# A branch hint at the top of every loop of a fused encoder layer

## The reference

```
mod = silu(c) @ w_mod + b_mod;  sh1, sc1, g1, sh2, sc2, g2 = split(mod, 6)
h = modulate(rms_norm(x), sh1, sc1)
u, q, k, v, f_logit = split(h @ w_in)
q, k = rms_norm(q) * q_gain, rms_norm(k) * k_gain
logf = log_sigmoid(f_logit + b_f)
pool_y = pool_mixer(u, ...)                       # trailing means, windows 2/4/8/16
s = q @ k.T / 8 + F[t] - F[s], masked             # F = cumsum(logf)
att = softmax(s) @ v
x = x + g1 * (concat(pool_y, att) @ w_out)
h2 = modulate(rms_norm(x), sh2, sc2)
y = x + g2 * (square(relu(h2 @ w_up)) @ w_down)
```

## Time and profile before

| | |
|---|---|
| median of 3 runs | 3430.89 us (3429.97 to 3432.27) |
| profiled execution | 3426.77 us, its span 3425.3 us |
| busy | PE 3118.1 us (91%), DVE 2067.2 (60%), ACT 1523.1 (44%), POOL 259.6 (8%) |
| mean granted TensorE clock | 0.953 of 2.4 GHz |

### The profile page before, as it was taken

How to read it: one execution, slowest core, us unless ns; L and a number is a source line. 1 busy time by engine, 2 the same in 40 slices (tenths; PEclk the granted TensorE clock), 3 DMA queues, 4 the chain that set the end, 5 groups by cost and what they waited for, 6 DMA issues and landing times. The chain is left out here.

```text
span 3425.3 us, 51085 instructions
## 1 busy us (share of the span) xinstructions
PE 3118.1 (91%) x17260; PEld 2675.8 (78%) x17260; DVE 2067.2 (60%) x3437; ACT 1523.1 (44%) x2561; POOL 259.6 (8%) x263
## 2 busy tenths in 40 slices
PE   4999998568599999999698899999999999999997
PEld 2999998145478787888486799899899888888886
DVE  3656764533288888889465455655655655565554
ACT  2344443023288888888222344344333333333331
POOL 0000000111111111112000000100100100020001
PEclk7999999689699999999899899999999999999999
DMA  5567565899543434330676643534543632243331
GB/s 193 192 221 247 194 230 179 266 298 320 164 119 84 120 85 106 96 96 12 190 222 196 202 131 127 195 124 129 190 133 124 210 103 92 93 177 117 98 98 50
DMA packets 373365, 532.73 MB, mean 156 GB/s; under 512 B 25488, under 2 KB 305560, under 8 KB 366553
## 3 DMA queue, kind: packets, MB, share of 16 engines
q1 hardware_dynamic: 361421, 487.37, 45.4%
q0 software_dynamic: 11808, 43.79, 3.5%
HBM read 410.69 MB, written 107.95 MB: 151 GB/s over the span
## 5 line engine op out<-in xcount | busy, mean ns | idle before, releaser
L2284 PE MATMUL c_psu<-c_hT,c_up_hi 128*128 128x384 f32 (+1 forms) x2560 | 711.1, 359 | 26.7 <-DVE c_up_lo L2207 19.0
L2284 PEld LDWEIGHTS c_psu<-c_hT,c_up_hi 128*128 128x128 f32 x2560 | 474.2, 189 | 72.9 <-issue 20.3
L2228 DVE TENSOR_TENSOR c_ff<-c_ff,c_psd 128x512 f32<-128x512 f32 x544 | 370.1, 686 | 246.9 <-PE c_psd L2297 244.4
L2284 PE MATMUL c_psu<-c_hT,c_up_lo 128*128 128x384 f32 (+1 forms) x1280 | 458.7, 358 | 0.0
L2168 ACT ACTIVATE c_relu<-c_psu 128x384 f32<-128x384 f32 (+1 forms) x160 | 85.3, 533 | 800.9 <-PE c_psu L2284 800.9
L2297 PE MATMUL c_psd<-c_dn_hi,c_a_hi 128*128 128x512 f32 x1088 | 424.5, 390 | 5.6 <-DVE c_ff L2228 5.6
L2297 PE MATMUL c_psd<-c_dn_hi,c_a_lo 128*128 128x512 f32 x1088 | 425.5, 391 | 0.0
L2297 PE MATMUL c_psd<-c_dn_lo,c_a_hi 128*128 128x512 f32 x1088 | 425.5, 391 | 0.0
L632 PE MATMUL p_psm<-p_whi,p_hT_hi 128*128 128x384 f32 (+1 forms) x952 | 321.8, 338 | 16.8 <-DVE p_wlo L525 10.2
L632 PE MATMUL p_psm<-p_whi,p_hT_lo 128*128 128x384 f32 (+1 forms) x952 | 316.2, 332 | 0.0
L632 PE MATMUL p_psm<-p_wlo,p_hT_hi 128*128 128x384 f32 (+1 forms) x952 | 311.9, 328 | 0.0
(11 more groups left out here) (229 smaller groups left out, 5340.9 us busy)
## 6 DMA issues: line engine op xcount, KB each, us to landing
c_up_raw<-in_w_up_dram SPq DMA_DIRECT2D x80, 1024.0 KB, 5.5
c_dn_raw<-in_w_down_dram SPq DMA_DIRECT2D x80, 1024.0 KB, 4.9
p_raw<-in_w_in_dram SPq DMA_DIRECT2D x24, 1536.0 KB, 7.4
s_krows<-in_cache_k_dram SPq DMA_DIRECT2D x16, 1536.0 KB, 7.0
s_vrows<-in_cache_v_dram POOLq DMA_DIRECT2D x16, 1536.0 KB, 7.7
o_wm<-in_w_mod_dram SPq DMA_DIRECT2D x16, 1024.0 KB, 7.3
q_split<-p_split SPq DMA_DIRECT2D x34, 384.0 KB, 2.3
k_split<-p_split SPq DMA_DIRECT2D x34, 384.0 KB, 2.4
```

What stands on the lines that cost most here:

```text
L2228: dve.tensor_tensor(out, out, ps_d[bank_of(u, p, wide)][:], ALU.add).then_inc(dn_free, 1)
L2284: done = pe.matmul(ps_u[g][:, 0:rows], w[p][:, k, f], x[:, k, 0:rows], start=begin, stop=end)
```

## The change

```diff
+def loop(eng, start, end):
+
+    return eng.bass.Fori(start, end, engines=bass.OrderedEngineSet([eng.engine]), hint_back_edge=True)
...
 def blocks(eng, body):
 
     body(0, 1)
-    with eng.Fori(1, BLOCKS - 1) as b:
+    with loop(eng, 1, BLOCKS - 1) as b:
...
     n = HEADS // 2
     body(0, False)
-    with eng.Fori(1, n - 1) as j:
+    with loop(eng, 1, n - 1) as j:
         body(j, False)
     body(n - 1, True)
...
         def over_steps(eng, b, unit):
 
-            with eng.Fori(0, STEPS // 2 - 1) as i:
+            with loop(eng, 0, STEPS // 2 - 1) as i:
...
```

More of the change, by code:

```diff
@@ L1468, in groups @@
             body(1)
-            with eng.Fori(2, STREAMS) as b:
+            with loop(eng, 2, STREAMS) as b:
                 body(b)
@@ L1786, in over_tiles @@
                 step(0, k)
-            with eng.Fori(1, N // 2 - 2) as i:
+            with loop(eng, 1, N // 2 - 2) as i:
                 for k in range(2):
@@ L2050, in over_blocks @@
         def over_blocks(eng, body):
-            with eng.Fori(0, SMALL) as b:
+            with loop(eng, 0, SMALL) as b:
                 body(b, False, False)
@@ L2099, in body @@
             def body(b, next_wide, last):
-                with sp.Fori(0, STEPS // 2 - 1) as i:
+                with loop(sp, 0, STEPS // 2 - 1) as i:
                     for p in range(2):
@@ L2113, in body @@
                     load_down(first, 0)
-            with sp.Fori(0, SMALL - 1) as b:
+            with loop(sp, 0, SMALL - 1) as b:
                 body(b, False, False)
@@ L2144, in body @@
                     load_x2(b + 1, next_wide)
-            with pool.Fori(0, SMALL - 1) as b:
+            with loop(pool, 0, SMALL - 1) as b:
                 body(b, False, False, False)
```

## The result

The changed kernel is slower: ratio 1.0044 of the kernel before, 95% interval 1.0028 to 1.0060, 15 us; medians of eight runs are 3443.76 us (3436.69 to 3451.45) and 3429.53 us (3420.01 to 3433.95). Its profiled span is 18.1 us longer.

The account below looks back on a forecast made before the run. TensorE carries the time; ScalarE's and VectorE's code stalls at the pair loop's jumps cap the gain at 16.55 us. Terms -8.7 + 0.6 = -8.1 us took the 3430.9 us median to 3423 us, range 3415 to 3442.

Parts of the forecast that it names:

- (a): All loops: the hints' own price, counted where TensorE waits for others, 6 stream and 4 pair rounds; 0.6 us slower.
- my upper end of 11.8: All loops: all 55 hints per engine exposed at 215 ns each would cost 11.8 us.
- (b): Pair loop's jump back: one of ScalarE and VectorE in time, the other wins 2.9 us; 8.7 us won over three jumps.
- the 0.7: Pair loop: chance that an engine's hinted fetch is in time, (20 - 5.8) / 20, from about six code pieces a round.
- (d): After the pair loop's jumps: TensorE goes on sooner, its slow clock goes with the stall, next loads unchanged; no separate term.
- my slower rival: Loop exits: hints displace the fetch of following code; 12.6 us on TensorE, 5.5 at the pairs' end; 3441 us, chance 0.30.
- (c): Other loops' back edges: nothing to win, TensorE's jump taking 0.3 us, SP and GpSimd hidden behind the matmuls.
- the hint does nothing: Pair loop: jumps stay at 5.8 us, hints cost 0.6 us; 3431.5 us, the same time; chance 0.11.

Follow-up runs that it names:

- unrolled kernel: Kernel before, no hints, the pair loop's four rounds written out on ScalarE and VectorE; 0.9954 of the kernel before, median 3412.49 us.
- placed kernel: Changed kernel with all its hints, ScalarE's pair loop moved to another place in its code; 0.9974 of the kernel before.

## Why the prediction was wrong

**What bounds the kernel** was right: the three jumps of ScalarE and VectorE in the pair loop were the code stalls that cost time, and 16.55 us their price. The unrolled kernel won 15.8.

**(a) The hints' price**, 0.6 us, can't be told from none in any single stage (1.0002 to 1.0008). All loops but the pairs together lost 8 us, between my 0.6 and my upper end of 11.8, but the placed kernel adds up without any such loss.

**(b) The jump back is the step that failed.** I said "one of the two is in time, the other wins half of its fetch, 2.9 us", 8.7 us in all. The first half is what happened: VectorE was in time. ScalarE won 1.2 us of 5.8 instead of 2.9: its first packet came 3.0 us after the branch as before, and moving the loop made it 5.5 of 5.8. I also took 2.9 us off TensorE's wait at each jump; its three waits shrank by 1.0 us in all, since two of them were no longer than 3.5 us before. The loop lost 4.8 us where I had it win 8.7. My way to the 0.7, six pieces of code on each engine in a round, was wrong too: half of the 12 packets hung on the jump. With fewer and longer pieces it would have come out higher, so this isn't what made me too hopeful.

**(d)** turned the sign in the loop. I wrote that "the slow clock after the stall goes with the stall". It does when the stall goes wholly (clock 1.00 in the unrolled run). With ScalarE still late it lasted 27.6 us behind the three waits instead of 13.2. Half of the 14.4 us more is 7.2 us, an estimate from above; less the 1.0 us of shorter waits it makes 6.2, and the loop lost 4.8. Why the low clock lasted longer is open: a wait of the same length was followed by 2.8 us of it in another execution.

**The exit** I left at nothing in my sum, and it measured 8.1 us. It was my slower rival: +10.0 us and 3441 foretold, +15 and 3443.8 measured. Its mechanism was there at the pair loop: with the hint TensorE's code from behind the loop came only after the exit. It cost 8.1 us where I had put 5.5 for VectorE and ScalarE, and 1.8 for TensorE, 7.3 in all. Its larger term, six more exits of TensorE at 1.8 us, did not show: in channel mixing TensorE had no wait for code at all. The rival came near the time partly by luck: it kept a gain of 8.1 us that wasn't there, and took 10.8 us for exits that cost nothing that shows.

**(c)** held: no other back edge changed. The rival "the hint does nothing" fell with VectorE's 0.6 us. The Trainium skill (Runtime: NRT & Kernel Launch, Instruction fetch mechanics) calls prefetch purely sequential; here a hint made it fetch a branch target, in time on VectorE (0.6 us after the branch), and left the code behind the loop late.

## What to carry to other kernels

Before hinting a loop, read branch to head on each engine: here only the loop whose code is brought in again each round had something to win. A hint is worth what the latest engine wins from it, and that depended on where the loop stands in the code; writing a loop of few rounds out on the engines that stall did at least as well (15.8 us against 13, no hint, no exit to pay). Ask what the hint's fetch displaces, and read the first 10 us behind the loop's end. A stall that only gets shorter need not win what it is shorter by, so read TensorE's wait and clock at every jump, not at the first alone, before counting a gain.

## What the runs showed of the hardware

- The same hint brought ScalarE to its loop's head 4.6 us or 0.3 us after the branch, by the loop's place alone; the place without the hint made 5.8 into 4.6.
- With the hint on TensorE the code behind the loop, brought in during the first round before (1164.6 us), came only after the exit: 3.9 us after the last branch with the hint on TensorE alone, 6.6 to 6.8 us where VectorE had it too.
- Late code at a loop's exit isn't additive over engines: the hint on TensorE alone cost 0.4 us, on VectorE alone 1.8, on both 9.0, each from one profile. Open why.
- Behind waits of 3.50 and 3.44 us in one execution TensorE's low clock lasted 2.8 and 9.4 us. The pair's period lay between 115.9 and 120.4 us in executions with a stall, while those without one gave 112.2 to 112.3.
